# Backward direction's state groups exchanged, angle tables moved and TensorE's front reordered in an S5, latent-attention and PEER layer

## The reference

```python
sh1, sc1, g1, sh2, sc2, g2 = modulation(cvec, w_mod, b_mod)     # silu(c) @ w_mod, 1024 x 6144
h = modulate(x, norm1, sh1, sc1)
u, c_q, c_kv, k_rope = split(h @ w_in, ...)                      # 512, 384, 256, 32 columns
ssm_out, state = s5_mixer(u, ...)       # 32 groups of 16, 64 states each, forward and backward
q, k, v = ...                           # from rmsnorm(c_q) and rmsnorm(c_kv)
x = x + g1 * (concat(ssm_out, attend(q, k, v)) @ w_out)
h2 = modulate(x, norm2, sh2, sc2)
x = x + g2 * peer(h2, w_query, sub_keys, u_table, v_table)
```

## Time and profile before

| | |
|---|---|
| median of 3 runs | 847.51 us (846.6 to 848.02) |
| span of the profiled execution | 845.6 us |
| TensorE busy | 709.4 us (84%), 3385 matmul records |
| DVE busy | 591.7 us (70%) |
| POOL busy | 369.8 us (44%), of it 299.0 us the issue of 256 gathers |
| ScalarE busy | 335.1 us (40%) |
| DMA | 321.74 MB, 268.45 MB of them by the gathers; mean 380 GB/s |

### The profile page before, as it was taken

One profiled execution on the slowest core, in us unless ns is written; L12 is line 12 of the kernel. 1 busy time (PEld: TensorE's weight loads), 2 busy tenths in 40 slices (PEclk: granted clock), 3 DMA queues, 4 the chain that ended last, 5 costly groups with the idle time before them and its releaser, 6 DMA issues. The chain is left out here.

```text
span 845.6 us, 10339 instructions
## 1 busy us (share of the span) xinstructions
PE 709.4 (84%) x3385; PEld 352.9 (42%) x3385; DVE 591.7 (70%) x1284; ACT 335.1 (40%) x995; POOL 369.8 (44%) x335
## 2 busy tenths in 40 slices
PE   3899999999978988899869887778787778778784
PEld 0586666655433455576524232223232223222221
DVE  7979623667995568958898756787687478644444
ACT  3423351345457324434344443343334333533331
POOL 3628900145334453344555445445445444445400
PEclk9999999999999999999989999999999999999998
DMA  9966696889999999999999999999999999999991
GB/s 353 411 211 218 224 399 249 314 301 396 396 416 336 422 421 423 395 420 421 421 420 421 421 420 422 421 422 422 421 421 422 422 421 422 423 419 422 422 421 70
DMA packets 50270, 321.74 MB, mean 380 GB/s; under 512 B 9948, under 2 KB 10652, under 8 KB 12200
## 3 DMA queue, kind: packets, MB, share of 16 engines
q0 software_dynamic: 36864, 268.45, 77.3%
q1 hardware_dynamic: 12984, 52.44, 16.0%
q10 hardware_dynamic: 368, 0.18, 0.1%
HBM read 318.77 MB, written 1.23 MB: 378 GB/s over the span
## 5 line engine op out<-in xcount | busy, mean ns | idle before, releaser
L840 PE MATMUL psum<-mem 128*128 128x512 f32 x952 | 469.2, 624 | 104.6 <-ACT mem L1227 103.3
L1500 POOL DMA_INDIRECT mem<-uv_table,small x256 | 299.0, 1168 | 352.3 <-PE psum L840 275.6
L1850 DVE CUSTOM_DVE_ANT_0 mem<-mem,h 128x1024 f32<-128x1024 f32 x256 | 311.6, 1225 | 176.1 <-DMA mem<-uv_table,small 170.2
L840 PEld LDWEIGHTS psum<-mem 128*128 128x128 f32 x952 | 170.9, 195 | 369.5 <-ACT mem L1227 223.2
L1216 ACT ACTIVATE small<-small 128x1 f32<-128x1 f32 x252 | 51.0, 202 | 298.2 <-DVE small L1850 293.1
L1227 ACT ACTIVATE mem<-consts,small 128x128 f32<-128x128 f32 x238 | 95.6, 402 | 7.9
L1221 ACT ACTIVATE small<-small 128x1 f32<-128x1 f32 x256 | 75.4, 295 | 26.3 <-issue 1.5
L787 PEld LDWEIGHTS psum<-hT,mem 128*128 128x128 f32 x352 | 42.5, 194 | 9.7 <-issue 7.2
L787 PE MATMUL psum<-hT,mem 128*128 128x128 f32 x352 | 42.9, 278 | 2.3 <-DMA mem<-w_query 2.3
L1417 POOL TENSOR_SCALAR small<-small 128x1 f32<-128x1 f32 (+1 forms) x9 | 5.2, 579 | 87.9 <-DVE small L1880 40.0
L509 PE MATMUL psum<-mem,scol 128*32 128x512 f32 x128 | 21.0, 735 | 16.0 <-DMA mem<-w_mod 15.8
(11 more groups left out here) (234 smaller groups left out, 671.2 us busy)
## 6 DMA issues: line engine op xcount, KB each, us to landing
mem<-w_mod SPq DMA_DIRECT2D x24, 1024.0 KB, 9.5
mem<-w_query SPq DMA_DIRECT2D x6, 1024.0 KB, 9.8
mem<-w_out SPq DMA_DIRECT2D x4, 1024.0 KB, 7.3
mem<-uv_table,small POOLq DMA_INDIRECT x256, 24.8
mem<-w_in_u SPq DMA_DIRECT2D x2, 1024.0 KB, 14.2
late<-w_query SPq DMA_DIRECT2D x2, 1024.0 KB, 9.6
mem<-w_in_qkv SPq DMA_DIRECT2D x2, 1008.0 KB, 13.0
mem<-w_ukv SPq DMA_DIRECT2D x1, 1024.0 KB, 8.1
```

What stands on the lines that cost most here:

```text
L840: mm = pe.matmul(bank(f"acc_{g}_{half}"), diag[:, pick % DEEP, :], row_of(pick)[:, D + 512 * half:D + 512 * half + 512], start=first, stop ...
L1500: pool.indirect_dma_start(row_of(pick), None, uv_table, bass.IndirectOffsetOnAxis(ap=idx[:, pick:pick + 1] if pick else first_idx, axis=0) ...
L1850: dve.tensor_tensor_reduce(out=row[:, 0:D], in0=row[:, 0:D], in1=h[:, pick // PICKS, :], scale=1.0, scalar=0.0, op0=ALU.mult, op1=ALU.add, ...
```

## The change

- The state groups of the backward direction change sides: what lay in partitions 0 to 63 lies in 64 to 127 and the other way about (the host-side packing `by_unit` and `by_state`, `x0`, `hlT`). `input_weights` and `s5_in` now issue their 64x64 products at four tile positions, forward ones at (0, 0) and (64, 64), backward ones at (0, 64) and (64, 0), and their two banks hold a direction each, where they held a real and an imaginary part. `s5_products` and `weights_evac` read them so. `y_carried(u)` is split into a forward and a backward half, with a semaphore between them.
- The angle table, four instructions of 1056 columns, moves from DVE to POOL, ahead of `rstdx`; the absolute value and both sines come earlier on ScalarE. `xrow` is made in two halves, and the second lag product's last step is moved behind `s5_products(0)`.
- `input_projection(0)` goes through k in the order 0, 4, 1, 5 and so on, with a wait for each pair of columns of hT; DVE makes the lower half and ScalarE the upper one.
- TensorE's calls from `quad_step(0, 5)` to `pair_step("a", 0)` stand in a new order, the banks with them. POOL's root of the latents goes behind `s5_last(1)`.
- SyncE issues `b_mod` earlier, all four `inputs_to_chunks` together, and all windows ahead of the loads of `mod1.4` to `mod1.7`.

The diff, with the rest left out:

```diff
-            for c in range(3):
+            for c in range(NC):
                 inputs_to_chunks(c)
...
-            inputs_to_chunks(3)
             for n in range(ORDER["mod1.1"], ORDER["mod1.4"]):
                 load(PAGES[n][0])
             for c in range(NC):
                 kernel_windows(c)
+            for c in range(NC):
                 load(f"mod1.{4 + c}")
...
             def input_weights(c):
...
+                pe.wait_ge(xpow_ready, 1 + c // 2)
+                outs = [start(f"W_{c}_{d}") for d in range(2)]
...
+                    for j in range(4):
+                        for d in range(2):
+                            at_ = 256 * r + 64 * j
+                            for e in range(2):
+                                es, hs = side_of(e), side_of(e ^ d)
+                                mm = pe.matmul(outs[d][es, at_:at_ + 64], xrow[hs, r, 8 * c + 4 * d + j, :, :].rearrange("p q k -> p (q k)"),
+                                               ident[hs, hs], start=True, stop=True, tile_position=(hs.start, es.start))
+                            if r == 1 and j == 3:
+                                finish(mm, f"W_{c}_{d}")
...
-                for k in range(KD):
+                for k in (0, 4, 1, 5, 2, 6, 3, 7):
                     arrived(f"in_u.{k // 4}")
+                    if c == 0 and k % 4 < 3:
+                        pe.wait_ge(high_ready if k >= 4 else low_ready, k % 4 + 1)
+                    elif c == 0:
+                        for g in range(G):
+                            wait_emptied(pe, f"xT_{g}_{k // 4}")
...
+                    for j in range(4):
+                        for d in range(2):
+                            at_ = 256 * r + 64 * j
+                            for e in range(2):
+                                es, hs = side_of(e), side_of(e ^ d)
+                                mm = pe.matmul(psum[hs, d, at_:at_ + 64], win[es, u, r, 4 * d + j, :],
+                                               chunks(ut[es, u, j, :].rearrange("p (g n) -> p g n", g=G), d),
+                                               start=True, stop=True, tile_position=(es.start, hs.start))
                 mm.then_inc(bu_ready, 1)
...
+            def y_carried(u, d):
+                if d:
+                    pe.wait_ge(forward_done, u + 1)
+                else:
+                    pe.wait_ge(sum_ready, 2 * u + 2)
                 out = psum[:, 4 + u % 2, :]
                 for j in range(4):
...
+                    a = 4 * d + j
+                    for r in range(2):
+                        for e in range(2):
+                            es, hs = side_of(e), side_of(e ^ d)
+                            mm = pe.matmul(out[es, 64 * j:64 * j + 64], ypow[hs, r, 8 * u + a, 1:5, :].rearrange("p k q -> p (k q)"),
+                                           chunks(view(u, r)[hs, a, :, 0:CHUNKS], d),
+                                           start=False, stop=j == 3 and d == 1 and r == 1, tile_position=(hs.start, es.start))
+                mm.then_inc(y_ready if d else forward_done, 1)
...
-            for k in range(6):
+            for k in range(5):
...
                     transposes(f"xT_{g}_{q}", [h[:, g, P * k:P * k + P] for k in range(4 * q, 4 * q + 4)])
+            quad_step(0, 5)
+            input_weights(0)
             quad_step(0, 6)
             quad_step(0, 7)
             wait_emptied(pe, "mq0")
             transposes("mcol", [modrow[:, 0, P * q:P * q + P] for q in range(4)])
-            input_weights(0)
             input_weights(1)
-            for name in ("xT_0_0", "xT_0_1", "xT_1_0", "xT_1_1"):
-                wait_emptied(pe, name)
             input_projection(0)
             input_projection(1)
             input_projection(2)
             s5_in(0)
             input_projection(3)
+            s5_in(1)
             input_weights(2)
-            latents(0, (0, 1))
-            s5_in(1)
+            quad_step(1, 0)
+            latents(0, (0,))
+            s5_in(2)
             input_weights(3)
-            latents(0, (2, 3))
-            quad_step(1, 0)
-            s5_in(2)
-            latents(0, (4, 5))
             kernels()
-            latents(0, (6, 7))
+            latents(0, (1, 2))
+            s5_in(3)
+            latents(0, (3, 4, 5, 6, 7))
             quad_step(1, 1)
-            s5_in(3)
-            quad_step(1, 2)
             y_local(0)
-            y_carried(0)
-            quad_step(1, 3)
+            y_carried(0, 0)
             pe.wait_ge(bu_used, NC)
             latents_turned(0)
+            y_carried(0, 1)
             y_local(1)
-            quad_step(1, 4)
+            y_carried(1, 0)
+            quad_step(1, 2)
             attention_queries(0, 0)
+            y_carried(1, 1)
             attention_queries(0, 1)
-            y_carried(1)
-            quad_step(1, 5)
-            attention_keys(0, 0, "kv")
             y_spread(0)
             y_spread(1)
+            y_local(2)
+            y_carried(2, 0)
+            quad_step(1, 3)
+            y_carried(2, 1)
+            attention_keys(0, 0, "kv")
+            y_local(3)
+            y_carried(3, 0)
+            quad_step(1, 4)
+            y_carried(3, 1)
             queries_turned(0)
             keys_turned(0, 0)
-            quad_step(1, 6)
-            y_local(2)
-            y_carried(2)
+            y_spread(2)
+            quad_step(1, 5)
             attention_scores(0, 0)
             attention_scores(0, 1)
-            y_spread(2)
-            y_local(3)
-            y_carried(3)
+            y_spread(3)
+            quad_step(1, 6)
             quad_step(1, 7)
-            y_spread(3)
...
+                for d in range(2):
+                    evacuate(win[:, c, :, 4 * d:4 * d + 4, :].rearrange("p r j n -> p r (j n)"),
+                             bank(f"W_{c}_{d}").rearrange("p (r m) -> p r m", r=2), f"W_{c}_{d}")
...
+            act.wait_ge(angle_ready, 1)
+            step(act.activation(tabs[:, 0, :, :], tabs[:, 1, :, :], ACT.Abs))
+            act.activation(tabs[:, 1, :, :], tabs[:, 1, :, :], ACT.Sin, scale=TWO_PI).then_inc(tab_ready, 1)
+            act.activation(tabs[:, 0, :, :], tabs[:, 0, :, :], ACT.Sin, scale=-TWO_PI, bias=half_pi[:, :]).then_inc(tab_ready, 1)
+            weights_evac(0)
             evacuate(modrow[:, 0, :], bank("mq0"), "mq0")
...
+            high_rows()
             weights_evac(1)
+            input_evac(0)
...
+            pool.wait_ge(turns_ready, 1)
+            angle, whole = tabs[:, 1, :, :], tabs[:, 0, :, :]
+            step(pool.tensor_tensor(angle, turns.unsqueeze(2).to_broadcast([P, DT, SL]), chunk_no.unsqueeze(1).to_broadcast([P, DT, SL]),
+                                    ALU.mult))
+            step(pool.tensor_scalar(whole, angle, MAGIC, None, ALU.add))
+            step(pool.tensor_scalar(whole, whole, MAGIC, None, ALU.subtract))
+            pool.tensor_tensor(angle, angle, whole, ALU.subtract).then_inc(angle_ready, 1)
...
                 if u + 1 < NC:
                     s5_sums(u + 1)
+                s5_turns(u)
+                s5_last(u)
                 if u == 1:
                     inverse_root(rstd_a[:, 0:2], ms_a[:, 0:2], [(0, 1, QR), (1, 2, KVR)], sqa_ready, 2, rstda_ready)
...
-                s5_turns(u)
-                s5_last(u)
...
-            tt(tabs[:, 1, :, :], turns.unsqueeze(2).to_broadcast([P, DT, SL]), chunk_no.unsqueeze(1).to_broadcast([P, DT, SL]), ALU.mult)
-            s_, c_ = tabs[:, 1, :, :], tabs[:, 0, :, :]
-            step(dve.tensor_scalar(c_, s_, MAGIC, MAGIC, ALU.add, ALU.subtract))
+            for two in range(2):
+                units = slice(16 * two, 16 * two + 16)
+                for r, op in ((0, ALU.subtract), (1, ALU.add)):
+                    tt(xrow[:, r, units], by_row(bm, r)[:, units], steps_back(cre)[:, units], ALU.mult)
+                    tt(sparer[:, units], by_row(bm, 1 - r)[:, units], steps_back(cim)[:, units], ALU.mult)
+                    ins = dve.tensor_tensor(xrow[:, r, units], xrow[:, r, units], sparer[:, units], op)
+                    if r == 0:
+                        step(ins)
+                    else:
...
-            for g in range(G):
-                for k in range(4):
+            for k in range(4):
+                for g in range(G):
...
-            tt(s_, s_, c_, ALU.subtract)
-            dve.scalar_tensor_tensor(c_, s_, -1.0, s_, ALU.mult, ALU.max).then_inc(angle_ready, 1)
...
-            dve.scalar_tensor_tensor(yb_, yb_, -1.0, spare, ALU.mult, ALU.subtract).then_inc(ypow_ready, 1)
...
+                    dve.tensor_tensor(work[u][:, k, :].rearrange("p (d j g n) -> p d j g n", d=2, j=4, g=G)[:, :, :, :, 1:SL],
+                                      psum[:, 0:2, 256 * r:256 * r + 256].rearrange("p d (j g n) -> p d j g n", j=4, g=G),
+                                      tabs[:, tab, 8 * u:8 * u + 8, 1:SL].rearrange("p (d j) n -> p d j n", d=2).unsqueeze(3)
```

(5 more changed lines are left out.)

103 lines of the change are left out of this document (35 added, 68 removed).

## The result

| | before | with the change |
|---|---|---|
| median | 847.31 us (846.6 to 848.02, 4 runs) | 870.71 us (869.57 to 871.94, 4 runs) |
| ratio, 95% interval | 1 | 1.0277 (1.0262 to 1.0292) |
| span of the profiled execution | 845.6 us | 867.8 us |
| first gather issued | 157.02 us | 180.09 us |
| from it to the end of the span | 688.6 us | 687.7 us |

The change is slower by 23.4 us, where the forecast said 15.7 with 870 as its upper end: the direction, the mechanism of the end and the last stretch were right, what happens ahead of the latents' transposes was not, and the sum was 7.7 us short.

A forecast was written before the change was run, and what follows sets the result against it. The prediction took the DMA gathers to bound the kernel from 200 us on, their start set by TensorE's full front. A pair 13.5 later, 0.5 for hlT copies and 1.7 for the clock made 847.5 + 15.7 = 863.2 us, range 852 to 870.

The forecast's parts named there:

- The end follows the first gather: DMA stretch from 200 us to the end: a first gather later by d ends the program later by d.
- Four quarters: input_weights and s5_in: passes fall from 31.7 to 17.9 ns, 0.88 us less a call, 7.0 for eight.
- Tables on POOL: Ahead of the columns: DVE loses 2.4 us of work, is held 4.0; first projection at 36.7, against 37.29.
- The transposes: Latents' transposes: TensorE arrives at 77.4, waits for POOL's root, and starts them at 82.5 instead of 83.86.
- the S5 chain is 4.7 early: DVE's second products ahead of the latents' transposes: at 55.5 instead of 60.17, so POOL's root can follow at 80.1.
- The transposes to the quads: From the latents' transposes to the last quad: 36.0 us instead of 26.95, including 6.2 of waits at spreads.
- SyncE's queue: mod2a.0 goes out behind quad (1,6); pair_step("a", 0) idles 5.9 us and starts at 124.4, 13.5 later.
- Behind it: From the pair to the first gather: 46.2 us as before, plus 0.5 for hlT copies and 1.7 for the clock.
- The order costs nothing: Rival on TensorE's order: its gains count if nothing waits, 839 us; chance 0.07.
- two quarters at a time: Rival on 64x64 products: weight loads don't overlap, a pass keeps 31.7 ns, 866 us; chance 0.14.
- DVE is not held: Rival on POOL's tables: all from the columns on is 4 us earlier, 859 us; chance 0.14.
- the load is in time: Rival at pair_step("a", 0): mod2a.0 lands as the quads end, 5.9 and 1.7 not lost, 856 us; chance 0.08.

The follow-up runs named there:

- e5: The change with POOL's four table instructions moved behind the decay tables and ScalarE's absolute value and sines behind input_evac(0): 869.24 us.
- e10: The kernel before with only the angle table moved to POOL and ScalarE's absolute value and sines early: 851.44 us, ratio 1.0047.
- e6: The change with the loads of mod1.2 and mod1.3 held back in SyncE's queue until kernels has ended: 870.59 us.
- e8: The kernel before with four quarters alone, and POOL's root of the latents ahead of s5_sums(2): 854.64 us, ratio 1.0087.
- e2: The change with the load of mod2a.0 put ahead of those of glu and out0.1 in SyncE's queue: 863.34 us.
- e4: The kernel before with only the exchanged groups, four-quarter products and y_carried as two halves back to back: 847.51 us, ratio 0.9996.
- e16: The same kernel as e4 run again in more rounds, against the kernel before: 848.62 us, ratio 1.0013.
- e9: The change with quads (1,6) and (1,7) ahead of y_spread(3), and mod2a.0 loaded ahead of glu and out0.1: 860.02 us.
- e3: The change with loops over d and j exchanged in input_weights and s5_in, so two quarters work at a time: 870.35 us.
- e1: The change with quads (1,6) and (1,7) put ahead of y_spread(3): 863.77 us.
- e7: The change with three steps of the latents put between s5_in(2), input_weights(3) and kernels: 871.25 us.
- e13: The change with the edits of e6 and e9, and POOL's root of the latents ahead of s5_turns(1): 859.89 us.
- e14: As e13, with both halves of y_carried(1) moved behind attention_queries(0, 1): 863.03 us.

## Why the prediction was right or wrong

- **The end follows the first gather.** Right, in all kernels.
- **Four quarters.** The term was right: 1.16 us for 64 passes is 18.1 ns against the 17.9 taken, 0.92 us less a call. The Trainium skill's 25 ns (TensorE: Matmul & The Clock Gate, Back-to-back issue gap) is no floor here. That the 7.0 us would be used up was right too, but not how: the forecast had TensorE early at the transposes and waiting there; it lost the time on the way.
- **Tables on POOL.** That DVE is held was right; which instructions, and how much, was not: "with the other two I take 4.0". Of the three one-tensor instructions counted, the first was held (1.97 us instead of 0.33), the other two were not (0.35 and 0.19 us, as before). What I had put at nothing, products with two tensors, made 5.2 of the 6.9 us ahead of `xrow`, and e5 showed the same of large ones. 1.5 of them are the decay tables, which had stretched `xrow` itself before, so the cost at the columns is 5.4 us against 4.0. The halves of `xrow` took 15.12 us (22.15 to 37.27) against 13.96 in e10 for the whole ones: 1.2, not 0.4. Together the columns were 2.2 us later than forecast (37.27, not 35.1), and the first projection came at 39.07, not 36.7: 2.4 us of the miss.
- **The transposes.** The step that failed most: 88.79, not 82.5, and with the late projection taken out 3.9 us of the miss. Two terms in it were wrong, and either alone makes it late. The first is TensorE's arrival, 77.4 by the forecast and 88.32 measured. From the projection on it took 49.2 us, not 40.7: two gaps put at nothing (5.0 us), and two stretches behind them largely at 1.2 GHz (granted 0.66 and 0.53), which took 4.83 us (61.02 to 65.85) and 5.77 us (73.00 to 78.77) where e6, at full clock, needed 3.18 and 3.03. So the latents were brought at 85.8. The second is "the S5 chain is 4.7 early": the second products came at 58.44, 1.7 early, and POOL took 7.9 us (76.89 to 84.79) for the turns and last states that had taken 6.1, now beside DVE's scan. Its root could begin at 84.8, not at 80.1. POOL's order alone gives 87.4 (e6); TensorE's lateness made it 88.8. The 4 to 5 us of waiting that were to show the step right were 0.47.
- **The wait's name.** The forecast saw `latent_ready` and passed over `bu_used` beside it. In the change the root is the later of the two (DVE's fourth products ended at 82.5); in e8 the other.
- **The transposes to the quads.** 36.0 forecast, 36.6 measured; spreads 1.20, 1.09 and 3.50 against 1.2, 1.3 and 3.5.
- **SyncE's queue.** 5.84 us of idle time against 5.9; e2 shows its cause.
- **Behind it.** 48.8 us from the pair to the gather, 2.6 more than before, against 2.2. The parts were off both ways: e4 and e16, which have the two copies of `hlT`, need 46.2 us, as before, so their 0.5 was nothing; e9, without the idle time, needs 46.5, so the idle time and the clock cost some 2.4, not 1.7. e2 has 47.5, with two waits for later loads in it (0.82 and 0.22).
- **The sum.** 2.4 + 3.9 + 0.6 + 0.4 = 7.3 us, which with 15.7 gives 23.0; the first gather moved by 23.1.
- **The rivals.** "The order costs nothing", "two quarters at a time", "DVE is not held" and "the load is in time" are refuted by the rows. x's root was 1.0 us late (18.43 against 17.39), not 5.5, as POOL's tables took 10.8 us, not 15.6. The upper end of 870 was too low: it held DVE's worst case, but not that TensorE and POOL would be late together.

## What to carry to other kernels

Follow the chain that crosses engines (here TensorE, DVE and POOL through the scans) before counting what one engine gains: work taken from TensorE ahead of a wait on that chain was worth nothing here (e4), and each wait that was removed let the next one show. Where two engines can each be late for the same instruction, price both: mending one alone (e6) gained nothing. Put consumers of such a chain behind other work, not right behind their producer, and look at what a load stands behind in its issue queue, since the load behind quad (1,6) went out 19 us later (124.12 against 104.95). Work moved from VectorE to GpSimd has to be priced with what VectorE loses meanwhile, products with two tensors above all: here 5.4 us lost ahead of the columns for some 5 us moved.

## What the runs showed of the hardware

- **TensorE stands without a wait, a little behind a packet of instructions.** The gaps marked "issue" end 2.4 to 2.8 us behind the half microsecond in which a 16 KB packet of the DMA queue of instructions starts. In the list of DMA queues the changed kernel has one from 70.5 us on (packets, MB, share):

```profile
q8 instruction: 1, 0.02, 12.2%
```

TensorE took up at 73.00. The pairs in the other runs: 57 and 59.58 (the change), 67.5 and 70.33 (e6), 35.5 and 38.31 (e4), 70.5 and 73.08 (e3), 69.5 and 71.88 (e1). With the change's calls a gap, where there is one, stands at the same pass (the rows count passes): behind 58 of the 64 of `input_weights(2)` and behind 99 of the 128 of `kernels`; in e7, with other calls ahead, behind 87. That TensorE waited for the packet is argued from this, and no run shows it by itself. Other packets have no gap (63.0 and 74.5 us in the change), and the size varies between executions: 3.37 us and none ahead of the projection in e4 and e16, which are one kernel, and 1.68, 3.56 and 3.48 in `kernels` in e6, e13 and e14, which are alike up to there. In the kernel before the one gap is 1.01 us. What asks for a packet, and when, no run shows.
- **VectorE beside GpSimd.** A product of 32 columns took 2.39 us instead of 0.19 and ended with POOL's table; two of 128 columns took 1.09 and 1.04 instead of 0.29 beside the decay tables; one of 1024 columns took up to 3.31 instead of 1.23 beside POOL's tables (e5). POOL's own instruction of 1056 columns took 2.3 to 3.8 us.
- **The clock.** The granted clock fell to 1.2 GHz (0.50) at some 123.1 us, behind the 3.50 us of idle time ahead of `y_spread(3)`, stayed there through the idle 5.84 us, and rose just before 137; the mean over 9.75 us from 131.25 on was 0.72. In e9, where the wait was 1.65 us and the idle time was gone, it stayed at 1.00 from 118 to 130 us. After the 3.55 us ahead of `input_weights(0)` two quads took 3.61 us at 0.50, where they took 1.92 in e3.
